# Attention steps by pairs of heads, with 64-row products by turns

## What is computed

```
# block 1: 8 heads with decay, 8 heads with a relative bias, head size 64
logits = q·kT/8 + F[t] - F[s]      (causal)                 o_a = softmax(logits)·v
logits = q·kT/8 + rel_bias[t - s]  (causal by 64-chunks, whole sequence in the band)  o_c = softmax(logits)·v
# block 2: window attention (8 heads; keys: 16 meta tokens, own and two earlier 64-chunks, one sink)
#          and gated linear attention (4 heads, key size 64, value size 128, chunks of 64)
o_intra = mask(qe·keT)·v;   o_inter = qe·S_chunk;   S_next = decay*S + kT·v
```

## Time and profile before

| | us |
|---|---|
| median of three runs | 2144.78 (2144.38 to 2148.55) |
| the profiled execution | 2148.04 |
| its span, first to last instruction | 2146.3 |
| TensorE busy in it | 2034.6 |
| VectorE, ScalarE busy | 1004.7, 727.4 |
| mean granted clock of TensorE | 0.976 of full speed |

### The profile page before, as it was taken

One profiled execution on the slowest core, in us unless ns is written; L12 is line 12 of the kernel. 1 busy time (PEld: TensorE's weight loads), 2 busy tenths in 40 slices (PEclk: granted clock), 3 DMA queues, 4 the chain that ended last, 5 costly groups with the idle time before them and its releaser, 6 DMA issues.

```text
span 2146.3 us, 26565 instructions
## 1 busy us (share of the span) xinstructions
PE 2034.6 (95%) x10813; PEld 1697.0 (79%) x10813; DVE 1004.7 (47%) x1340; ACT 727.4 (34%) x948; POOL 24.3 (1%) x45
## 2 busy tenths in 40 slices
PE   5999999996999999989999999899999999999997
PEld 2788877873777778869999999688887787888885
DVE  7678753435555552254444322666323444444322
ACT  3444443423454442242222212445323332222211
POOL 0000000000000000000000000000000000000000
PEclk9999999998999999999999999999999999999999
DMA  6643213220222222312222222111112222222221
GB/s 264 213 148 128 99 40 119 98 98 0 79 90 105 78 79 89 105 40 98 78 98 81 79 94 89 71 59 40 42 59 97 86 91 85 91 98 92 82 94 65
DMA packets 34846, 195.43 MB, mean 91 GB/s; under 512 B 3680, under 2 KB 3696, under 8 KB 19552
## 3 DMA queue, kind: packets, MB, share of 16 engines
q1 hardware_dynamic: 29008, 173.55, 23.0%
q0 software_dynamic: 5776, 21.02, 2.9%
HBM read 192.46 MB, written 2.10 MB: 91 GB/s over the span
## 4 chain that ended last, share of the span: by engine, by line
PE 83%; DVE 10%; ACT 3%; issue 2%; DMA 1%; ACTq 0%; SPq 0%; DVEq 0%
PE PS L567 82%; DVE W_lo L1546 2%; ACT W_hi L1114 1%; PE PS L697 1%; DVE INV L1590 1%; DVE N L1595 1%; DMA A_low<-in_wada 1%; DVE T L1985 1%; DVE T L1976 1%; ACT L1114 1%; DVE A_high L2019 1%; ACT T L1114 0%; DMA ring<-in_wada 0%; ACT H_hi L1114 0%; DVE H_lo L1578 0%
## 5 line engine op out<-in xcount | busy, mean ns | idle before, releaser
L567 PE MATMUL PS<-H_hi,W_hi 128*128 128x512 f32 (+1 forms) x1976 | 634.3, 355 | 57.6 <-DVE H_lo L1578 20.5
L567 PE MATMUL PS<-H_hi,W_lo 128*128 128x512 f32 (+1 forms) x1976 | 635.0, 355 | 0.0
L567 PE MATMUL PS<-H_lo,W_hi 128*128 128x512 f32 (+1 forms) x1976 | 632.5, 354 | 0.0
L1546 DVE TENSOR_TENSOR W_lo<-W_raw,W_hi 128x2048 fp32r<-128x2048 f32 (+2 forms) x170 | 353.1, 2077 | 325.8 <-ACT W_hi L1114 325.2
L567 PEld LDWEIGHTS PS<-H_hi,W_hi 128*128 128x128 f32 x1976 | 351.6, 192 | 121.2 <-issue 42.8
L1114 ACT ACTIVATE W_hi<-W_raw 128x2048 fp32r<-128x2048 f32 (+2 forms) x170 | 295.5, 1738 | 322.1 <-PE PS L567 321.3
L567 PEld LDWEIGHTS PS<-H_hi,W_lo 128*128 128x128 f32 x1976 | 351.0, 192 | 49.8 <-issue 0.2
L567 PEld LDWEIGHTS PS<-H_lo,W_hi 128*128 128x128 f32 x1976 | 350.1, 191 | 50.0 <-issue 0.2
L567 PE MATMUL PS<-G_hi,W_hi 128*128 128x512 f32 (+1 forms) x704 | 209.6, 338 | 1.3 <-DVE W_lo L1546 1.3
L567 PE MATMUL PS<-G_hi,W_lo 128*128 128x512 f32 (+1 forms) x704 | 210.2, 339 | 0.0
L567 PE MATMUL PS<-G_lo,W_hi 128*128 128x512 f32 (+1 forms) x704 | 209.3, 338 | 0.0
(11 more groups left out here) (246 smaller groups left out, 2169.4 us busy)
## 6 DMA issues: line engine op xcount, KB each, us to landing
W_raw<-in_wts SPq DMA_DIRECT2D x119, 1024.0 KB, 4.7
W_raw<-in_wdown SPq DMA_DIRECT2D x48, 704.0 KB, 4.0
ring<-in_wada POOLq DMA_DIRECT2D x32, 512.0 KB, 3.8
A_high<-in_wada SPq DMA_DIRECT2D x6, 1024.0 KB, 18.0
A_low<-in_wada SPq DMA_DIRECT2D x2, 1024.0 KB, 10.8
X<-in_xT SPq DMA_DIRECT2D x2, 1024.0 KB, 10.4
X<-in_xT POOLq DMA_DIRECT2D x1, 2048.0 KB, 9.0
out<-N SPq DMA_DIRECT2D x8, 256.0 KB, 2.1
```

Of the source, the lines that this page charges most:

```text
L567: return nc.tensor.matmul(*a, **kw)
L1546: vector.tensor_tensor(W_lo[:, c.odd, 0:size], W_raw[:, c.odd, 0:size], W_hi[:, c.odd, 0:size].bitcast(FP32), ALU.subtract).then_inc(w_lo, 1)
```

## The change

The units are put into another order: unit t is query block i = (t % 8) // 2 of head 2*(t // 8) + t % 2, so that two neighbouring units are the same block of two heads, one on partitions 0 to 63 and one on 64 to 127. In an even step TensorE issues the scores of units t and t+1 together, the 64-row products of the two by turns, into the two score banks; in an odd step it issues none. The wait ahead of them is for the exponential of unit t-1. Transpositions, WOVEN and the other engines' order within a step stay as they are.

The value products go by **phases** of four units (two heads, two query blocks): PT and PTW hold two heads of 256 queries instead of one of 512, and a phase writes two 256-column halves of PVOUT. ScalarE's side copy and VectorE's sum of the two output parts are then two instructions of 256 columns for each phase, instead of one of 512 for each head. The window attention is changed in the same way (`win_scores` and its waits as in the front; `win_output` is new). In the gated linear attention `gla_scores` and `gla_out` take the two heads by turns, and `gla_out` waits for both heads' AM at its start.

```diff
-            PT_hi = sb("PT_hi", [P, NB, SEQ], F32R, over)
-            PT_lo = sb("PT_lo", [P, NB, SEQ], F32R, over)
+            PT_hi = sb("PT_hi", [P, 2, NB, 2 * P], F32R, over)
+            PT_lo = sb("PT_lo", [P, 2, NB, 2 * P], F32R, over)
...
         def unit(t):
 
-            n, i = divmod(t, NB)
+            n, i = 2 * (t // (2 * NB)) + t % 2, t % (2 * NB) // 2
             h = n % HEADS
             return n, h // 4, h % 4 // 2, h % 2, i
 
         def win_unit(t):
 
-            n, i = divmod(t, NB)
-            return n, n // 2 + 4 * (n % 2), n // 2, n % 2, i
+            pair, half, i = t // (2 * NB), t % 2, t % (2 * NB) // 2
+            return 2 * pair + half, pair + 4 * half, pair, half, i
+
+        def win_cols(i):
+
+            return ((0, P), (P, 2 * P), (0, 2 * P), (2 * P, 2 * P))[i]
+
+        def win_values(phase):
+
+            if phase % 2 == 0:
+                return (0, 0, 0, 2 * P), (1, 2 * P, P, P)
+            return (1, 0, 0, P), (2, P, 0, 2 * P), (3, 3 * P, P, P)
...
             def front_scores(t):
-                n, g, pair, half, i = unit(t)
-                h, w, r, q = n % HEADS, P * (i + 1), rows_of(half), slice(i * P, (i + 1) * P)
-                o = score_bank(t)
-                mm(o[:, 0:w], QH[g][r, pair, q], KH[g][r, pair, 0:w], start=True, stop=False)
-                mm(o[:, 0:w], QL[g][r, pair, q], KH[g][r, pair, 0:w], start=False, stop=False)
-                mm(o[:, 0:w], QH[g][r, pair, q], KR[g][r, pair, 0:w], start=False, stop=n >= HEADS)
-                if n < HEADS:
-                    mm(o[:, 0:w], PICK[r, h:h + 1].to_broadcast([HEAD, P]), F2[r, 0:w], start=False, stop=True)
-                    return mm(o[:, i * P:w], ident_b, causal_b, start=False, stop=True, skip_group_check=True)
-                bias = BAND[:, h, P:2 * P] if i == 0 else BAND[:, h, :]
-                return mm(o[:, max(i - 1, 0) * P:w], exch, bias, start=False, stop=True, skip_group_check=True)
+
+                pair = [(score_bank(u), *unit(u)) for u in (t, t + 1)]
+                i = pair[0][5]
+                w, q = P * (i + 1), slice(i * P, (i + 1) * P)
+                fox = pair[0][1] < HEADS
+                for a, (left, right) in enumerate(((QH, KH), (QL, KH), (QH, KR))):
+                    for o, n, g, p, half, _ in pair:
+                        r = rows_of(half)
+                        mm(o[:, 0:w], left[g][r, p, q], right[g][r, p, 0:w], start=a == 0, stop=a == 2 and not fox)
+                if fox:
+                    for o, n, _, _, half, _ in pair:
+                        r = rows_of(half)
+                        mm(o[:, 0:w], PICK[r, n:n + 1].to_broadcast([HEAD, P]), F2[r, 0:w], start=False, stop=True)
+                for o, n, _, _, _, _ in pair:
+                    if fox:
+                        last = mm(o[:, i * P:w], ident_b, causal_b, start=False, stop=True, skip_group_check=True)
+                    else:
+                        h = n - HEADS
+                        bias = BAND[:, h, P:2 * P] if i == 0 else BAND[:, h, :]
+                        last = mm(o[:, max(i - 1, 0) * P:w], exch, bias, start=False, stop=True, skip_group_check=True)
+                    last.then_inc(sem("f_scores"), 1)
+
+            def front_values(phase):
+
+                n, g, pair, _, i0 = unit(phase * NB)
+                for half in range(2):
+                    for j in range(i0 + 2):
+                        c0 = max(j - i0, 0) * P
+                        for m, part in enumerate((PT_hi, PT_lo)):
+                            last = mm(PS[:, PVOUT, half * 2 * P + c0:(half + 1) * 2 * P], VHL[g][:, j, 2 * pair + half, :],
+                                      part[:, half, j, c0:2 * P], start=j == 0 and m == 0, stop=j == i0 + 1 and m == 1)
+                last.then_inc(sem("f_pv"), 1)
...
             def front_steps():
 
                 for t in range(STEPS):
                     v = t - 3
                     if v >= 0 and v % NB == NB - 1:
-                        n, g, pair, half, _ = unit(v)
+                        n, phase = unit(v)[0], v // NB
                         pe.wait_ge(sem("f_lo"), v + 1)
                         pe.wait_ge(sem("f_out_lo"), 3 * (n // 4) + 3)
-                        if n >= 1:
-                            pe.wait_ge(sem("f_sum"), n)
-                        for j in range(NB):
-                            values = VHL[g][:, j, 2 * pair + half, :]
-                            for m, part in enumerate((PT_hi, PT_lo)):
-                                last = mm(PS[:, PVOUT, j * P:SEQ], values, part[:, j, j * P:SEQ], start=j == 0 and m == 0,
-                                          stop=j == NB - 1 and m == 1)
-                        last.then_inc(sem("f_pv"), 1)
-                    if t < UNITS:
-                        n = t // NB
+                        if phase >= 1:
+                            pe.wait_ge(sem("f_sum"), 2 * phase)
+                        front_values(phase)
+                    if t < UNITS and t % 2 == 0:
+                        n = unit(t)[0]
                         if t == 0:
                             pe.wait_ge(sem("fox_decay"), 2)
                         if t == HEADS * NB:
@@ -685,8 +711,8 @@
                         if t % (4 * NB) == 0:
                             pe.wait_ge(sem("f_out_lo"), 3 * (n // 4) + 2)
                         if t >= 2:
-                            pe.wait_ge(sem("f_prob"), t - 1)
-                        front_scores(t).then_inc(sem("f_scores"), 1)
+                            pe.wait_ge(sem("f_prob"), t)
+                        front_scores(t)
...
+            def win_output(phase):
+
+                for half in range(2):
+                    o = PS[:, PVOUT, half * 2 * P:(half + 1) * 2 * P]
+                    for m, part in enumerate((PTM_hi, PTM_lo)):
+                        mm(o, VW[0:META, NB, half, :], part[:, half, :], start=m == 0, stop=False)
+                    values = win_values(phase)
+                    for n, (j, at, to, w) in enumerate(values):
+                        for m, part in enumerate((PTW_hi, PTW_lo)):
+                            last = mm(o[:, to:to + w], VW[:, j, half, :], part[:, half, at:at + w],
+                                      start=False, stop=n == len(values) - 1 and m == 1)
+                last.then_inc(sem("att_pv"), 1)
...
                     pe.wait_ge(sem("am_ready"), 2)
-                for hh in range(2):
-                    r = rows_of(hh)
-                    for n in range(NB):
-                        t0 = META + n * P
+                for n in range(NB):
+                    for hh in range(2):
+                        r, t0 = rows_of(hh), META + n * P
                         last = mm(PS[:, 4 + hh, n * P:(n + 1) * P], TB[r, m, t0:t0 + P], TA[r, m, t0:t0 + P], start=True, stop=True)
-                    last.then_inc(sem("gla_scored"), 1)
+                        if n == NB - 1:
+                            last.then_inc(sem("gla_scored"), 1)
 
             def gla_out(m):
                 bank = 6 - 2 * m
-                for hh in range(2):
-                    h, r = 2 * m + hh, rows_of(hh)
-                    pe.wait_ge(sem("am_ready"), h + 1)
-                    for n in range(NB):
+                pe.wait_ge(sem("am_ready"), 2 * m + 2)
+                for n in range(NB):
+                    for hh in range(2):
+                        h = 2 * m + hh
                         mm(PS[:, bank + hh, n * P:(n + 1) * P], LV[:, n, h * P:(h + 1) * P], AM[:, hh, n, :], start=True, stop=True)
-                        for c in (2 * n, 2 * n + 1):
-                            t0 = META + c * CHUNK
+                    for c in (2 * n, 2 * n + 1):
+                        for hh in range(2):
+                            r, t0 = rows_of(hh), META + c * CHUNK
                             last = mm(PS[:, bank + hh, c * CHUNK:(c + 1) * CHUNK], S[r, m, c, :], TA[r, m, t0:t0 + CHUNK],
                                       start=False, stop=True, skip_group_check=True)
                 last.then_inc(sem("og_raw"), 1)
...
-                        n, half = v // NB, v // NB % 2
-                        act.wait_ge(sem("f_pv"), n + 1)
-                        if n >= 2:
-                            act.wait_ge(sem("f_sum"), n - 1)
-                        activate(OSIDE[rows_of(half), :], PS[rows_of(1 - half), PVOUT, :], ACT.Copy).then_inc(sem("f_side"), 1)
+                        phase, c = v // NB, v // NB % 2 * 2 * P
+                        act.wait_ge(sem("f_pv"), phase + 1)
+                        if phase >= 2:
+                            act.wait_ge(sem("f_sum"), 2 * phase - 2)
+                        for half in range(2):
+                            ins = activate(OSIDE[rows_of(half), c:c + 2 * P],
+                                           PS[rows_of(1 - half), PVOUT, half * 2 * P:(half + 1) * 2 * P], ACT.Copy)
+                        ins.then_inc(sem("f_side"), 1)
...
```

(67 more changed lines are left out.)

64 lines of the change are left out of this document (32 added, 32 removed).

## The result

The changed kernel takes 2114.43 us (median of four runs, 2113.02 to 2115.54) against 2145.65 before: 31.2 us less, a ratio of 0.985 with a 95% interval of 0.9835 to 0.9869. The forecast was 2120 (2105 to 2139), faster. The profiled execution took 2113.68 us, span 2111.9.

The account below looks back on a forecast made before the run. TensorE, busy 95% of the span, was taken as the bound. Gross gains of 40.2 us less waits of 6.3 (fox), 2.7 (band) and 6.8 (window) gave 24.4 us, 2144.8 to 2120; range 2105 to 2139.

Parts of the forecast that it names:

- Shared entry and exit, and overlap: Fox, band, window: paired heads share 64-row entries and exits and overlap; gross gains 12.7, 13.6 and 6.4 us.
- 0.9 of each: Fox, band, window: share of the hidden second-half products counted as gained, 8.5 + 6.4 + 4.9 = 19.8 us.
- The bias term: Band heads: two two-pass fp32 bias products in a row expose first weights once, 0.19 us per pair, 3.0 us.
- Turns as the cause of the overlap: 64-row score products: two heads' products on different halves, issued by turns, overlap; 19.8 us in the attention stages.
- Waits in the front: Fox and band: short odd steps make TensorE wait behind VectorE's splits and modulation products; 6.3 and 2.7 us lost.
- The modulation: Fox stage: 24 modulation products take the slack of about twelve odd steps, 0.3 us each, 3.6 us lost.
- The window stage: Window attention: forecast unchanged, 6.8 us of waits eating a gross gain of 6.4.
- The 0.3 us in each of 16 odd steps: Window stage: odd transpositions come directly, so each odd step waits 0.3 us, 4.8 us in all.
- GLA: Gated linear attention: grouped output passes and alternated scores save about 7.5 us, somewhat more if less falls into low clock.
- Missing overlap: Rival, all 64-row stages: fp32r products on different halves don't overlap; net gain 9 us, 2136; chance 0.10.
- The evacuation rival: Rival: VectorE's and ScalarE's serial chain makes 48 step pairs wait, 34 us; net 6, 2139; chance 0.12.
- The slower rival: Rival: odd-step waits bring low-clock stretches, loss of 50 us against 40 gained, 2155; chance 0.08.

Follow-up runs that it names:

- e2_units: Changed kernel with each head's 64-row products in series and closed at once by its own 128-row bias or mask product: 2150.24 us.
- e10_win_old: Changed kernel with the window stage as it was before the change: 2112.72 us.
- e1_series: Changed kernel with all 64-row products of the first head before those of the second, in front and window attention: 2115.72 us.
- e9_gla_series: Changed kernel with the gated linear attention's 64-row products in series by head instead of by turns, groups still shared: 2116.81 us.
- e4_small_mod: Changed kernel with each of VectorE's woven modulation products on 64 of its 1024 columns: 2107.54 us.
- e5_gla_only: Kernel before with only the gated linear attention's changed order put in: 2128.63 us.
- e3_gla_old: Changed kernel with the gated linear attention's scores and outputs in the order of before: 2129.06 us.

## Why the prediction was right

- **Shared entry and exit, and overlap.** This step was right, in mechanism and size. TensorE's busy time fell by 13.7, 11.3 and 6.1 us in the three stretches; forecast were 12.7, 13.6 and 6.4. The experiment that takes the terms away gives back 27.8 us of busy time in fox and band for a forecast of 26.9 (e2_units). The "0.9 of each" for fp32r, taken from one fp32 row, held: pairs of 384 columns start 0.17 us apart, as single products do in e2_units. The Trainium skill (page "TensorE: Matmul & The Clock Gate", section "Measured speedup vs the span model") has 3.07x for four row tiles, which would have made the sum smaller; for two halves the measurement decides for nearly the full factor. The bias term was too large: 0.97 against 2 x 0.53 is 0.09 us a pair, 1.4 us and not 3.0. In the window stage the 6.1 flatters, since the clock rose from 0.97 to 0.98; against the same unpaired stage at 1.00 (e10_win_old) the gross gain is about 4.7.
- **Turns as the cause of the overlap.** Here the reasoning was wrong without harm: I tied the overlap to the alternation, and it comes from the two heads' products standing within one block (e1_series, e9_gla_series).
- **Waits in the front.** Fox 5.8 us against 6.3, band 1.5 against 2.7. That VectorE's long instructions would make them was right; place and make-up were half right, so the close size is partly luck. I costed only splits between the even and the odd unit, and the dearest waits, ahead of odd transpositions, came behind an odd unit, where I had found none: two of 1.2 us in fox and one of 0.9 in band behind a W_lo. A third of 1.2 us came behind the band tables' 2.3 us product (T, at 164.22), which was not in the sum; it needed the modulation too, since it goes in e4_small_mod. The modulation made 2.1 us, that wait among them, and not 3.6; I had also put all 24 of its products into fox, where the trace before has 19. Front together, 2128.63 (e5_gla_only) to 2112.72 (e10_win_old) = 15.9 us; forecast 17.3.
- **The window stage** unchanged: right (e10_win_old), but with both halves of the balance too large: 4.7 gained instead of 6.4, and 3.7 us of waits instead of 6.8. The 0.3 us in each of 16 odd steps did not come. Only three waits stand ahead of odd transpositions, two of 0.2 us and one of 2.4; two of 1.4 stand ahead of scores and three of 0.5 to 0.9 ahead of value products.
- **GLA.** The term that was mis-sized: forecast about 7.5 us, measured 14.6 (e3_gla_old) and 17.8 (e5_gla_only). The work at an even clock was right: the groups came at 1.24 us (forecast 1.22), the scores saved 0.57 each (0.55), 7 us by their starts. The clock was not. I had written "somewhat more" and counted 5.5 us lost within the two passes as I had cut them. In that same trace the low clock lasted from 1542.1 to 1549.2 and from 1573.0 to 1583.3, some 8.5 us lost, and all of it went. This miss is larger than the whole 5.6 us between 2120 and 2114; the front, 1.4 us under its forecast, missed the other way.
- **Rivals.** Missing overlap is refuted by rows of the trace. The evacuation rival, which the Trainium skill speaks for ("TensorEngine Tiling (Array Packing)", section "PSUM Bottleneck"), is real but not the bound: 11 of the 31 us of TensorE time saved in the three stretches came back as waits, 42% of it in fox, 13% in band and 60% in the window stage, where with the clock it was about all. The slower rival did not occur in the change. e2_units ended slower, with the low clock but with hardly more idle time.

## What to carry to other kernels

Count how often TensorE changes between 64-row (or 16-row) and 128-row products, not only the products: each block cost 0.28 us here beyond its columns, and two half-height products on different partitions in one block took the time of one; their order within four or so made no difference, a full-height product between them did. Then look what must be done within the step that has become short: a pairing takes away a step of slack, and long instructions of the evacuating engines (here 2.3 us) decide what is given back. Where TensorE runs at the low clock in a stage, its price belongs in the sum of an edit that changes that stage's order, and it is read to the end of the low clock, not of the stage. Here it doubled the GLA's gain.

## What was not expected of the hardware

- Half-height products that stand four and four in the program are started in pairs, fp32r and fp32 (e1_series, e9_gla_series). With eight passes and then eight only the last few overlap: 1.44 us from the first start to the last of the 16, against 0.89 by turns.
- The GLA output passes ran at a mean clock of 0.84 and 0.83 (two profiles) with blocks of two 128-row and four 64-row passes, and at 1.00 (eleven profiles) with groups of four and eight, at 1.24 us instead of 2.0 for the same work. TensorE was busy without a gap in both (43.33 of 43.33 us, 30.67 of 30.67).
- Waits alone did not decide the low clock. The window stage had none with 5.4 us of idle time (e5_gla_only) and 17 us of it with 6.4 (e2_units).
